# Reordering the state-space preparation of layer 0 in a two-layer diffusion block

## The reference

```python
p_lat = a_lat @ w_in                  # columns: f (Fourier), u (state space), ga, gb (gates)
h_l = diag_scan(bu_l, lam_bar, lam_dt, h_c[:, -1])      # two directions, 32 groups, 64 complex states
y_lat = y_lat + flip(jnp.einsum('blgp,ghp->blgh', h_l, c_mat).real)
y_a = fourier_mix(p[..., :OFF_SSM]) @ w_four            # 2D FFT
y_b = (y_s @ w_glu_a) * jax.nn.sigmoid(y_s @ w_glu_b)
return (g_a * y_a + g_b * y_b) @ w_out
```

## Time and profile before

| | |
|---|---|
| median of 3 runs | 2102.3 us (2099.48 to 2104.02) |
| profiled execution, span | 2109.0 us |
| PE busy | 2035.3 us (97%) |
| DVE busy | 1399.7 us (66%) |
| ACT busy | 940.9 us (45%) |
| DMA | 529.30 MB, mean 251 GB/s |
| granted TensorE clock, mean | 0.978 |

### The profile page before, as it was taken

How to read it: one execution, slowest core, us unless ns; L and a number is a source line. 1 busy time by engine, 2 the same in 40 slices (tenths; PEclk the granted TensorE clock), 3 DMA queues, 4 the chain that set the end, 5 groups by cost and what they waited for, 6 DMA issues and landing times.

```text
span 2109.0 us, 24695 instructions
## 1 busy us (share of the span) xinstructions
PE 2035.3 (97%) x10138; PEld 1539.4 (73%) x10138; DVE 1399.7 (66%) x1873; ACT 940.9 (45%) x859; POOL 0.2 (0%) x4
## 2 busy tenths in 40 slices
PE   5999899999999999999989999999999999999997
PEld 2456364447777777788887888888888888888886
DVE  5675536662222323646268898888988889898986
ACT  2212112121221221321227777777777777676775
POOL 0000000000000000000000000000000000000000
PEclk8999999989999999999989999999999999999998
DMA  9432694332435431368528999899998999999994
GB/s 401 84 133 107 199 247 183 140 109 95 184 140 219 160 150 70 120 200 200 180 120 317 373 353 371 340 364 369 360 371 332 369 360 363 359 346 369 360 364 158
DMA packets 83841, 529.30 MB, mean 251 GB/s; under 512 B 23056, under 2 KB 49552, under 8 KB 52752
## 3 DMA queue, kind: packets, MB, share of 16 engines
q1 hardware_dynamic: 62976, 508.65, 65.5%
q10 hardware_dynamic: 20752, 19.05, 2.6%
HBM read 509.39 MB, written 18.28 MB: 250 GB/s over the span
## 4 chain that ended last, share of the span: by engine, by line
PE 90%; DVE 4%; DMA 3%; ACT 1%; issue 1%; SPq 0%; DVEq 0%; ACTq 0%
PE ps L1692 19%; PE ps L2121 14%; PE ps L2106 14%; PE ps L2107 14%; PE ps L1701 6%; PE ps L1705 6%; PE ps L1708 6%; PE ps L1635 2%; PE ps L1926 1%; DMA GR<-in_w_mod 1%; PE ps L2052 1%; DVE WL L1517 1%; DMA mring<-in_moe_down 1%; PE ps L2035 1%; PE ps L1934 1%
## 5 line engine op out<-in xcount | busy, mean ns | idle before, releaser
L1517 DVE TENSOR_TENSOR WL<-mring,WH 128x2048 fp32r<-128x2048 f32 x336 | 755.2, 2287 | 108.2 <-ACT WH L949 108.0
L949 ACT ACTIVATE WH<-mring 128x2048 fp32r<-128x2048 f32 x336 | 626.1, 1913 | 139.2 <-PE ps L2121 117.4
L2106 PE MATMUL ps<-WH,XGh 128*128 128x512 f32 x896 | 355.9, 397 | 2.4 <-ACT WH L949 2.4
L2107 PE MATMUL ps<-WH,XGl 128*128 128x512 f32 x896 | 351.5, 392 | 0.0
L2121 PE MATMUL ps<-WL,XGh 128*128 128x512 f32 x896 | 221.7, 390 | 0.0
L1311 DVE TENSOR_TENSOR ringl<-ring,FWH 128x4096 fp32r<-128x4096 f32 (+2 forms) x21 | 82.3, 3917 | 187.6 <-ACT FWH L794 187.6
L1692 PE MATMUL ps<-aT,ring 128*128 128x512 f32 (+1 forms) x576 | 199.8, 507 | 0.0
L2106 PEld LDWEIGHTS ps<-WH,XGh 128*128 128x128 f32 x896 | 169.3, 189 | 36.7 <-issue 2.5
L794 ACT ACTIVATE FWH<-ring 128x4096 fp32r<-128x4096 f32 (+2 forms) x21 | 67.8, 3231 | 285.4 <-DMA ring<-in_ffn_gu 152.9
L2107 PEld LDWEIGHTS ps<-WH,XGl 128*128 128x128 f32 x896 | 169.5, 189 | 33.9
L2121 PEld LDWEIGHTS ps<-WL,XGh 128*128 128x128 f32 x896 | 168.2, 188 | 34.9
(11 more groups left out here) (291 smaller groups left out, 2234.6 us busy)
## 6 DMA issues: line engine op xcount, KB each, us to landing
mring<-in_moe_gate SPq DMA_DIRECT2D x56, 2048.0 KB, 9.6
mring<-in_moe_up SPq DMA_DIRECT2D x56, 2048.0 KB, 9.6
mring<-in_moe_down SPq DMA_DIRECT2D x56, 2048.0 KB, 9.5
ring<-in_w_mod SPq DMA_DIRECT2D x23, 2048.0 KB, 8.1
ring<-in_w_in SPq DMA_DIRECT2D x11, 2048.0 KB, 10.4
ring<-in_ffn_gu SPq DMA_DIRECT2D x11, 2048.0 KB, 10.9
cks<-CW ACTq DMA_DIRECT2D x16, 512.0 KB, 3.1
ring<-cks SPq DMA_DIRECT2D x4, 2048.0 KB, 12.2
```

Of the source, the lines that this page charges most:

```text
L949: nc.scalar.activation(WH[buf][:, o], mring[t % MRING][:, o], ACT.Copy).then_inc(high_done, 1)
L1517: V.tensor_tensor(WL[buf][:, o], mring[t % MRING][:, o], WH[buf][:, o].bitcast(F32), ALU.subtract).then_inc(low_done, 1)
L2106: mm(out_, ah, WH[buf][:, o:o + 512], start=(first and q == 0), stop=False)
L2107: mm(out_, al, WH[buf][:, o:o + 512], start=False, stop=False)
```

## The change

The functions stay; calls move, and buffers are laid out anew.

- `poles()` and the first half of `tables(0)`, now `powers(0)`, are called before the first modulation columns, not behind the first norm.
- Layer 0's input powers have five BP buffers (`NBP = 5`), not two. `turn(0, 0..3)` follow u directly, then ga 0, `turn(0, 4..7)`, E, and ga 1 to 7 behind E.
- All eight `masked` run at once into eight LB buffers.
- The lags go one at a time: behind f 2, f 3, dft1 of blocks 2 and 3, dft2 of block 2, gb 0, 1 and 2. `store_reads` on ScalarE follow the same places. There are still two CW buffers, but one Gs.
- `mod_columns(1)` moves behind the lags. `raw` of layer 1 is issued behind gb 3, not gb 4. `turn(1, 0)` goes between gb 5 and gb 6, `turn(1, 1)` behind gb 7; the ya products keep six turns.
- Of layer 1's BW buffers, BWs takes turns 0, 1, 2, 4, 6 and BW1 3, 5, 7.
- The side products take other banks: transforms 5 to 7, lags bank 4.

The banks and buffers:

```diff
+NBP = 5
+TURNED = ((0, 1, 2, 4, 6), (3, 5, 7))
...
         side([("dft1", 0, m, t) for m in range(4) for t in range(4)]
-             + [("dft2", 0, m, s) for m in range(4) for s in range(2)])
-        side([("lag", 0, mh) for mh in range(2)])
+             + [("dft2", 0, m, s) for m in range(4) for s in range(2)], (5, 6, 7))
+        side([("lag", 0, mh) for mh in range(2)], (4,))
+        side([("turn", 1, n, r) for n in range(2) for r in range(2)])
...
+        LBs = [sb(masks, f"LB{i}", [P, 4, 2, 32]) for i in range(ITS)]
...
+        BPh = [sb(prep, f"BPh{i}", [P, 2, 4, P]) for i in range(NBP - 1)]
```

ScalarE, behind the copies of f, dft1, dft2 and gb in this order:

```diff
+                    if l == 0 and m >= 2:
+                        store_reads(0, m - 2)
...
+                    if l == 0 and m >= 2:
+                        store_reads(0, m)
...
+                    if l == 0 and m == 2:
+                        store_lags(0, 0)
+                        store_reads(0, 4)
...
+                    evac(("gb", l, m), G2[:, m, t0:NT], ACT.Sigmoid, n)
+                    if l == 0 and m < 3:
+                        store_reads(0, 5 + m)
                     if l == 0 and m == 3:
-                        store_lags(0, 0)
-                    evac(("gb", l, m), G2[:, m, t0:NT], ACT.Sigmoid, n)
-                    if l == 0 and m < 4:
-                        for i in range(2 * m, 2 * m + 2):
-                            store_reads(0, i)
-                        for i in range(2 * m + 2, 2 * m + 4):
-                            if i < ITS:
-                                masked(0, i)
-                    if l == 0 and m == 4:
                         store_lags(0, 1)
                         act.wait_ge(b_masked, 2 * ITS)
                         act.dma_start(raw[:].rearrange("p a r c h -> p (a r c h)"), a["bc"][1]).then_inc(raw_in, 16)
```

VectorE, at the first norm and behind the scan:

```diff
                     invert(0, 0)
+                    poles()
+                    powers(0)
                     dve.wait_ge(vectors_in, 2 * 16)
                     mod_columns(0)
...
                 if l == 0:
-                    mod_columns(1)
                     for k in range(ITS):
                         out_powers(0, k)
-                        if k == 5:
+                        if k == 4:
                             lag_rows(0, 0)
                     lag_rows(0, 1)
+                    mod_columns(1)
+                    powers(1)
                     tables(1)
+                    in_powers(1, 0)
+                    in_powers(1, 1)
```

TensorE, behind u, and behind the f products (in the same way as on ScalarE for the transforms and gb):

```diff
-                    mod_turn(4)
-                    for k in range(4):
-                        gate_a(k)
-                        turn(0, 2 * k)
-                        turn(0, 2 * k + 1)
-                        if k == 1:
-                            mod_sums(5)
-                        if k == 2:
-                            mod_turn(5)
+                    for i in range(4):
+                        turn(0, i)
+                    gate_a(0)
+                    for i in range(4, ITS):
+                        turn(0, i)
...
+                        if l == 0 and m >= 2:
+                            lags(0, m - 2)
```

More of the change, by code:

```diff
@@ L562, in ring_load @@
                     for b in range(2):
-                        sp.wait_ge(bw_stored[b], 16 * 2 * (key[2] + 1))
+                        sp.wait_ge(bw_stored[b], 16 * sum(n_ < 4 * (key[2] + 1) for n_ in TURNED[b]))
                 if key[0] == "ck":
@@ L695, in masked @@
             def masked(l, n):
-                b = n % 2
                 c0 = 8 * (n // 2) + 4 * (n % 2)
                 act.wait_ge(bbar_ready, l + 1)
-                if l == 0 and n == 0:
-                    act.wait_ge(u_stored, 16 * 4)
+                if n == 0:
+                    for r in range(2):
+                        _, done, _, at, _ = place(("turn", l, ITS - 1, r))
+                        act.wait_ge(done, at + 1)
                 if l == 1 and n == 0:
[L703 to L709, removed]
+                    for b in range(2):
+                        act.wait_ge(bw_stored[b], 16 * len(TURNED[b]))
                 for c in range(2):
-                    nc.scalar.activation(LBs[b][:].rearrange("p g r (c h) -> p c r g h", c=2)[:, c],
+                    nc.scalar.activation(LBs[n][:].rearrange("p g r (c h) -> p c r g h", c=2)[:, c],
                                          raw[:, 0, :, c0:c0 + 4, :], ACT.Copy,
@@ L717, in turned @@
                 mh, q = n // 4, n % 4
-                BW = (BWs, BW1)[n % 2]
-                if l == 1 and n >= 2:
-                    act.wait_ge(bw_stored[n % 2], 16 * (n // 2))
+                b = 0 if n in TURNED[0] else 1
+                BW = (BWs, BW1)[b]
+                if l == 1 and TURNED[b].index(n):
+                    act.wait_ge(bw_stored[b], 16 * TURNED[b].index(n))
                 for r in range(2):
@@ L881, in _ @@
                 if l == 0:
-                    for m in range(8):
-                        turned(1, m)
+                    for i in range(2, ITS):
+                        turned(1, i)
                     mod_rows(10)
@@ L1143, in power, with powers @@
                 link(V.tensor_tensor(zt[:, k0 + by - 1:k1 + by, 1, :], x3, x4, ALU.add))
-            def tables(l):
+            def powers(l):
                 link(V.tensor_copy(zt[:, 0], lam1[:, :, 32 * l:32 * l + 32]))
@@ L1216, in out_powers @@
                             dve.wait_ge(y_stored[mh], 16 * CHUNK)
-                if n == 1:
-                    for r in range(2):
-                        _, done, _, at, _ = place(("turn", l, ITS - 1, r))
-                        dve.wait_ge(done, at + 1)
-                    if l == 1:
-                        for bw in bw_stored:
-                            dve.wait_ge(bw, 16 * ITS // 2)
                 if n >= 2:
@@ L1348, in _ @@
                 if l == 0:
-                    poles()
                     dve.wait_ge(con_in, 16)
@@ L1652, in turn @@
             def turn(l, n):
-                b = n % 2 if l == 0 else 0
+                b = n % NBP if l == 0 else 0
                 pe.wait_ge(powers_made, ITS * l + n + 1)
@@ L1673, in lags @@
                         rows = slice(32 * g, 32 * g + 32)
-                        last = mm(bank[rows, o:o + P], LBs[b][:, g, r, :], CWs[b][:, r, g, s_:s_ + P],
+                        last = mm(bank[rows, o:o + P], LBs[n][:, g, r, :], CWs[b][:, r, g, s_:s_ + P],
                                   start=(q == 0 and r == 0), stop=(q == 3 and r == 1), skip_group_check=True)
@@ L1844, in first_transform @@
                             product(("dft1", l, m, t), [(uF[:, m, P * t:P * t + P], con[:, C_CS:C_CS + 256])], 256)
+                        if l == 0 and m >= 2:
+                            lags(0, m)
                 if l == 1:
@@ L1889, in _ @@
                         product(("dft2", l, m, s), pairs, 256)
+                    if l == 0 and m == 2:
+                        lags(0, 4)
                 if l == 0:
@@ L1942, in _ @@
                     product(("ya", l, m), [(w[:, k, P * m:P * m + P], uF[:, k, t0:NT]) for k in range(MB)], n_)
-                    if l == 0:
-                        turn(1, m)
+                    if l == 0 and 1 <= m < 7:
+                        turn(1, m + 1)
                 if l == 0:
```

87 lines of the change are left out of this document (42 added, 45 removed).

## The result

| | before | after |
|---|---|---|
| median of the runs, us | 2102.07 (4 runs, 2099.48 to 2104.02) | 2118.26 (4 runs, 2116.7 to 2121.17) |
| span of the profiled execution, us | 2109.0 | 2119.4 |
| TensorE busy, us | 2035.3 (97%) | 2033.6 (96%) |

The ratio of after to before is 1.0076, with a 95% interval of 1.0062 to 1.0089, so 13.0 to 18.7 us more. The two profiled spans differ by only 10.4 us, because before's profiled execution lies above all of its timed runs. What the change does is therefore read at a place that both kernels pass with the same work done: the glub products of layer 0 start at 338.40 us before and at 352.38 after, 14.0 us later, and the sums of the second norm at 457.25 and 471.23, again 14.0 later.

A forecast was written before the change was run, and what follows sets the result against it. TensorE was taken as the bound, 90% of the chain. Terms -10.8 + 0.4 + (10.2 + 2.4) + (8.8 + 2.4) = +13.4 us on the profiled 2109.0 gave 2122.4, less 6.7 to the runs' median, about 2115; range 2099 to 2122.

The forecast's parts named there:

- The likeliest case: Both new waits appear, before lags 3 and before layer 1's first turn: +13.4 us, 2115; chance 0.60.
- Old waits: gb waits for read powers, 3.24 and 2.87 us, go with their slow clock; two ya turn waits go: 10.8 us gained.
- the rival without waits: Neither new wait appears, before lags 3 or before layer 1's first turn: 2093; chance 0.13.
- Store 1 at F + 15, lags 3 at F + 19.2, wait 10.2: F ends the last f product; store 1 meets two 2 MB loads, TensorE waits 10.2 us, slow clock 2.4.
- Raw at T + 17.1, wait 8.8: T ends gb 3; raw queues behind the lag store beside loads; layer 1's first turn waits 8.8 us, clock 2.4.
- One for one: DMA queues alternate single packets, so a store of many small packets lands about when the loads do, F + 15.
- Poles first at no cost, bounded by 0 and 0.5: Before the first norm: modulation columns start 0.5 us late, but 1.9 us of slack hides it; cost 0.
- Turn copies, +0.4: Four turns together: ScalarE's copies need 2.06 us per two turns against TensorE's 2; 0.4 us lost, bounds 0 and 1.5.
- E helps nobody directly: Layer 0: E and the scan come 22 us earlier, but read powers 0 and 1 are needed only at the third f product.
- The worse rival: Late landings pass on to read powers 6 and raw, some 4 us each: +13.4 + 8, 2124; chance 0.08.
- First alone: Only the wait before lags 3 appears, since raw comes early: +3.1 us, 2105; chance 0.12.
- second alone: Only layer 1's first-turn wait; store 1 precedes loads (many-packet turns: 3 to 5 us over free landing): +0.8, 2103; chance 0.07.

The follow-up runs named there:

- Experiment 3: Changed kernel with store 1 issued behind f 2 and raw of layer 1 loaded behind gb 2: 2093.87 us, ratio 0.9954 to before.
- experiment 5: Changed kernel with two issues behind gb 3 exchanged, raw of layer 1 ahead of the lag store: 2109.13 us, ratio 1.0023 to before.
- Experiment 8: Changed kernel with store 1 writing its 512 KB as 128 rows of 4 KB instead of 1024 of 512 bytes: 2111.8 us, ratio 1.004 to before.
- experiment 9: Experiment 3's kernel with only the poles ahead, the powers moved behind the first norm: 2090.71 us, ratio 0.9938 to before.
- experiment 7: Experiment 3's kernel with two buffers of input powers instead of five: 2108.72 us, ratio 1.0027 to before.
- experiment 4: Changed kernel with SyncE waiting until store 1 has landed before it issues w_mod: 2109.56 us, ratio 1.0025 to before.
- experiment 6: Experiment 3's kernel with poles and powers back behind the first norm: 2098.06 us, ratio 0.9975 to before.
- experiment 1: Changed kernel with store 1 issued behind f 2, together with the first store, not behind f 3: 2105.26 us, ratio 1.0005 to before.
- experiment 2: Changed kernel with raw of layer 1 loaded behind gb 2, one product earlier; lag store stays behind gb 3: 2106.8 us, ratio 1.001 to before.
- experiment 10: Experiment 3's kernel unchanged, run once more beside experiment 9: 2093.21 us, ratio 0.9946 to before.

## Why the prediction was right, and where it was off

The likeliest case came out: two new waits of about 10 us at the places named, each released by the transfer named, with 1.2 GHz behind. 2118 lies within the range and within the case's own 2109 to 2119. At the glub products the change came out at +14.0, against the +13.4 forecast. That this is so close is in part luck: the two new waits with their slow clock took 1.5 us more than forecast (25.3 against 23.8), and the 1.35 won inside E, which no term of the sum had, nearly cancels it. By its steps:

- **Old waits, -10.8.** Right: no idle from gb 0 to gb 3 and the clock up. Experiment 3, which has the gains without the new waits, came at 2093.87; the rival without waits had 2093. At the glub products it is 11.9 us ahead of before (326.54 against 338.40): the 10.8 less what the longer wait before E took, and the 1.35 inside E.
- **Store 1 at F + 15, lags 3 at F + 19.2, wait 10.2.** F was 179.84. Landed at F + 15.8, lags at F + 20.0, wait 10.74. Store and load were issued within 0.01 us of each other, so the neighbour in before carried over nearly unchanged; the other store behind it, for which I had taken 0.8 off, made no difference.
- **Raw at T + 17.1, wait 8.8.** T was 249.27. VectorE's tables began at T + 18.2, and the wait was 10.23. This is the term of the sum that was most mis-sized, by 1.4 us. About 0.5 of it is raw's issue behind the lag store's (249.74), which I had not counted; the landing was 17.7 from there. The path itself, small packets in front in the same queue, is shown by experiment 5.
- **One for one, not many small packets a turn.** Right. The rule of the Trainium skill (DMA: Bandwidth & Descriptors, section Queues, rings and completion order), a whole packet of typically 9 to 17 descriptors at each turn, is not borne out here: the counts of the two queues agree in each microsecond from 184 to 192, where by that rule one queue would move its 9 to 17 on an engine while the other moved none. The late landing alone would not have told. The 3 to 5 us that the prediction gives for the rival left out that a turn of the loads' queue would be as long by the same rule: 216 packets in 8 us are 13.5 on each of 16 engines, so 9 to 17 of them take 5 to 10 us, an estimate from the page's figure and this rate. Experiment 8's 9.0 us fits one for one and does not by itself exclude the other.
- **Poles first at no cost, bounded by 0 and 0.5.** The number held, the norm started 0.22 us later than in before (39.37 against 39.15), but by luck. The 1.9 us of slack that I read between the columns and the norm belonged to TensorE's running at 1.2 GHz in that execution. In after's it ran at 2.4 GHz there and was done 2.0 us earlier. VectorE came later than forecast, too, with its columns at 38.73 instead of 37.75, since its reciprocal had ended 1.2 us later than in before. So VectorE with its powers held TensorE back: idle of 4.34 us before u against 2.08. The edit cost 0.2 us against the execution of before and 2.3 against what that one could do, as experiment 9 shows.
- **Five buffers hide the input powers.** Right, and the price of taking them away (experiment 7) was the 10 to 15 expected.
- **Turn copies, +0.4.** The wait before E is 1.31 against 1.09, so 0.2.
- **E helps nobody directly.** Of the early scan right; but E itself lost its gap of 1.35 us. What the gap was isn't shown: the profile calls it "issue". In before E ran beside loads that took 0.98 to 0.99 of the DMA engines' time (111 to 118 us), in after and experiment 3 at the same clock beside a share of 0.02 and without the gap. Layer 1's E runs beside loads in both kernels (shares of 0.94 to 1.10) and has such a gap in both, 1.40 us in before and 1.24 in after. In these four places the gap goes with the loads; by which path is open. That instructions came late because of the loads would fit, and was not tried.
- **The worse rival** (late landings passed on, 2124) did not happen in after, but experiment 4 is its mechanism: a store that meets the loads one step later, 3.21 us of wait.
- **First alone, second alone** were put at 2105 and 2103, and measured 2106.8 and 2105.3. The runs of before beside them stood at 2104.37 instead of 2102.3. By differences to before they were put at +3.1 and +0.8, and measured +2.4 and +0.9.

## What to carry to other kernels

A small transfer that someone waits for must not be issued together with the weight loads: issue it ahead of them or count its packets, since here its landing went by their number against the loads' and not by its bytes alone. When stores or loads are moved in program order, list for each new place what the other queues issue at that moment and what stands before it in its own; here two moved lines turned a gain of 11 us into a loss of 16. Slack in front of an engine is only as large as in the executions in which its releaser runs at its full clock.

## What was not expected of the hardware

- 512 KB in 512-byte rows land after 3.1 us in free queues and after 15.8 beside 4 MB of loads; the same bytes in 4 KB rows after 9.0.
- An idle of 2.55 us (experiment 5) had no slow clock behind it, while the 2.57 of experiment 6, which ended 3.7 us after a wait of 1.28, had (the turn took 1.97 us instead of 1.04), as had the 2.87 of before. The waits of 2.87 us and more in before, after and experiments 1, 2, 4, 5 and 8 cost 1.6 to 3.0 us on top of themselves (least behind the 3.21 of experiment 4, most behind the 11.05 of experiment 2, where the transform row took 13.19 us instead of 10.63).
- TensorE's clock in the first 40 us differs between executions: 0.50 in 34.5 to 37 us for before and experiment 3, 1.00 for after, experiment 9 and experiment 10, which is experiment 3's kernel. Which it will be was not settled; between before and after it was worth 2.0 us at TensorE's last step ahead of u (done at 39.0 and 37.0).
